# Zero matmuls ahead of the waits in the first retention head of a decoder trunk

## What is computed

```python
def retention_mixer(h, w_in, w_out):       # h = rmsnorm(x, g[0]), 512 x 1024
    proj = h @ w_in
    q, k, v, gate = jnp.split(proj, [H*RET_DK, 2*H*RET_DK, 2*H*RET_DK + H*RET_DV], axis=-1)
    q = rotary(q, pos)
    k = rotary(k, pos) * (RET_DK ** -0.5)
    ...
    def step(state, inp):                  # chunks of 128 tokens
        qc, kc, vc = inp
        inner = jnp.einsum('bhnd,bhmd->bhnm', qc, kc) * decay_mask[None]
        out = jnp.einsum('bhnm,bhme->bhne', inner, vc)
        ...
    y = rms_unit(y) * jax.nn.silu(gate)
    return y @ w_out
```

## Time and profile before

| | |
|---|---|
| time, median of 3 runs | 1361.86 us (1361.46 to 1362.64) |
| time of the profiled execution | 1362.79 us |
| its span, first to last instruction | 1360.8 us |
| PE busy | 1326.5 us, 97% of the span |
| DVE, ACT, POOL busy | 903.3, 555.8, 85.3 us |
| mean granted clock of PE | 0.992 of full speed |
| PE's share of the chain that ended last | 89% |

### The profile page before, as it was taken

The page is one execution under the profiler, slowest core; times in us unless marked ns, Lnnn a source line. Parts: engine busy times, 40 slices in busy tenths (PEclk is TensorE's granted clock), DMA queues, the critical chain, the costliest instruction groups (busy, mean ns, idle before and its releaser), DMA issues.

```text
span 1360.8 us, 19429 instructions
## 1 busy us (share of the span) xinstructions
PE 1326.5 (97%) x8028; PEld 1183.7 (87%) x8028; DVE 903.3 (66%) x951; ACT 555.8 (41%) x681; POOL 85.3 (6%) x129
## 2 busy tenths in 40 slices
PE   5989999999999999999999999999999999999997
PEld 4768888888889899999888889899788999998886
DVE  4977767774357788887233666667578888874342
ACT  4253434343334443443222455456354444443231
POOL 1000000000011000000000211221120000000001
PEclk8989999999999999999999999999999999999999
DMA  7161424226434333323224123223224233323221
GB/s 248 47 215 60 135 70 142 83 62 245 172 109 125 95 93 110 119 82 125 93 92 139 32 75 105 76 71 124 93 91 126 78 109 94 109 62 125 92 93 62
DMA packets 101055, 145.57 MB, mean 107 GB/s; under 512 B 3659, under 2 KB 77643, under 8 KB 100980
## 3 DMA queue, kind: packets, MB, share of 16 engines
q1 hardware_dynamic: 90816, 137.18, 31.0%
q10 hardware_dynamic: 10164, 7.32, 1.7%
HBM read 138.17 MB, written 8.41 MB: 108 GB/s over the span
## 4 chain that ended last, share of the span: by engine, by line
PE 89%; DVE 5%; POOL 2%; ACT 1%; issue 1%; DMA 1%; SPq 0%; ACTq 0%; DVEq 0%; POOLq 0%
PE ps L1819 29%; PE ps L1821 28%; PE ps L1820 28%; PE ps L2146 1%; DMA raw<-in_ret_w_in 1%; PE ps L1865 1%; POOL rstd L710 1%; PE ps L2168 1%; PE ps L2167 1%; PE ps L2156 0%; PE ps L2031 0%; ACT junk L794 0%; DVE tmp L1236 0%; DVE tmp L1254 0%; POOL spare_lo L734 0%
## 5 line engine op out<-in xcount | busy, mean ns | idle before, releaser
L1216 DVE TENSOR_TENSOR w_lo<-raw,w_hi 128x2048 fp32r<-128x2048 f32 (+1 forms) x69 | 143.4, 2078 | 202.0 <-ACT w_hi L785 170.1
L1819 PE MATMUL ps<-h_hi,w_hi 128*128 128x256 f32 (+1 forms) x688 | 224.8, 327 | 0.0
L1821 PE MATMUL ps<-h_hi,w_lo 128*128 128x256 f32 (+1 forms) x688 | 223.9, 325 | 0.0
L1820 PE MATMUL ps<-h_lo,w_hi 128*128 128x256 f32 (+1 forms) x688 | 223.9, 325 | 0.0
L1819 PE MATMUL ps<-w_hi,act_hi 128*128 128x512 f32 x536 | 209.5, 391 | 1.1 <-ACT tmp L1026 0.8
L1821 PE MATMUL ps<-w_hi,act_lo 128*128 128x512 f32 x536 | 208.8, 390 | 0.0
L1820 PE MATMUL ps<-w_lo,act_hi 128*128 128x512 f32 x536 | 208.7, 389 | 0.0
L785 ACT ACTIVATE w_hi<-raw 128x2048 fp32r<-128x2048 f32 x44 | 84.2, 1913 | 174.2 <-PE ps L1821 171.6
L1819 PEld LDWEIGHTS ps<-h_hi,w_hi 128*128 128x128 f32 x688 | 131.0, 190 | 10.7
L1821 PEld LDWEIGHTS ps<-h_hi,w_lo 128*128 128x128 f32 x688 | 131.0, 190 | 10.7
L1820 PEld LDWEIGHTS ps<-h_lo,w_hi 128*128 128x128 f32 x688 | 131.0, 190 | 10.4
(11 more groups left out here) (253 smaller groups left out, 2947.0 us busy)
## 6 DMA issues: line engine op xcount, KB each, us to landing
raw<-in_ffn_w_down SPq DMA_DIRECT2D x22, 1024.0 KB, 5.1
x<-in_ret_w_in SPq DMA_DIRECT2D x13, 1024.0 KB, 5.2
raw<-in_ffn_w_up SPq DMA_DIRECT2D x24, 512.0 KB, 4.4
raw<-in_ffn_w_gate SPq DMA_DIRECT2D x24, 512.0 KB, 3.9
raw<-in_ret_w_in SPq DMA_DIRECT2D x10, 1024.0 KB, 5.2
raw<-in_ret_w_out SPq DMA_DIRECT2D x8, 1024.0 KB, 5.1
raw<-in_diff_w_in SPq DMA_DIRECT2D x8, 1024.0 KB, 5.6
tmp<-in_ffn_w_gate SPq DMA_DIRECT2D x12, 512.0 KB, 3.9
```

The source lines that it names most:

```text
L1216: nc.vector.tensor_tensor(out_ap, whole, high.bitcast(F32), ALU.subtract).then_inc(done, 1)
L1819: nc.tensor.matmul(out_ap, a_hi, b_hi, start=start, stop=False, skip_group_check=shared)
L1820: nc.tensor.matmul(out_ap, a_hi, b_lo, start=False, stop=False, skip_group_check=shared)
L1821: return nc.tensor.matmul(out_ap, a_lo, b_hi, start=False, stop=stop, skip_group_check=shared)
```

## The change

Matmuls of a tile of zeros are added on PE. The tile, `zeros`, is bf16, 128 partitions by 512 columns, and one DVE instruction sets it to 0 near the start. One call of `fill(b, n)` issues n matmuls of 128x512 into bank b, each with a start and a stop of its own, and nothing reads the result. No instruction is removed and none of the others is reordered. There are 56 such matmuls: 14 before the first transposes, 6 between the first two transposed blocks, 8 ahead of and 8 behind the last transposed block, 4 ahead of the wait for `bias_cp`, and 16 ahead of T3 in head 0, behind the wait for `ret_u2_made`.

```diff
+            zeros = sb("zeros", [P, S], BF16, ret)
...
             nc.vector.memset(rel[BUCKETS:BUCKETS + 1, :], MASKED).then_inc(set_up, 1)
+            nc.vector.memset(zeros[:], 0.0).then_inc(zeros_made, 1)
...
+            def fill(b, n):
+
+                for _ in range(n):
+                    nc.tensor.matmul(bank(b), zeros[:, 0:P], zeros[:], start=True, stop=True)
+
+            pe.wait_ge(zeros_made, 1)
+            fill(6, 14)
             pe.wait_ge(const_in, 16)
             turn_rows(0, 0)
+            fill(6, 6)
             turn_rows(0, 1)
...
             left_product(0, "B11", "a", True, between=first_rows)
+            fill(6, 8)
             turn_rows(0, 3)
+            fill(6, 8)
             pe.wait_ge(ret_p1_copied, 2)
             left_product(0, "B21", "a", False)
...
             mm.then_inc(bias_mm, 1)
             pe.wait_ge(h_split, ST)
+            fill(0, 4)
             pe.wait_ge(bias_cp, 1)
             columns(unit(0, "Q"), unit(0, "Q") % 3, (6, 7))
...
                 pe.wait_ge(ret_u2_made, h + 1)
+                if h == 0:
+                    fill(2, 16)
                 left_product(h, "T3", "b", True)
```

More of the change, by code:

```diff
@@ L223, in build @@
         first_row = sem("first_row")
+        zeros_made = sem("zeros_made")
         first_hi_made = sem("first_hi_made")
```

## The result

The changed kernel takes 1364.41 us (median of 16 runs, 1362.07 to 1367.15), against 1361.76 us (median of 16 runs, 1360.23 to 1362.77) for the kernel before. The ratio is 1.0023, with a 95% interval of 1.0016 to 1.0030, so the kernel became slightly slower, by 2.65 us. The forecast was 1362.6 in a range of 1359.5 to 1365.2. The profiled execution took 1366.44 us, its span is 1364.4 us, 3.6 more than before.

What follows compares the result with a forecast made beforehand. PE bounds the kernel, busy 1326.5 of 1360.8 us, with early waits and cold clock costing time. Profiled: 1362.79 - 2.9 + 3.5 - 0.6 = 1362.8; median: 1362.5; forecast 1362.6, own range 1361.2 to 1363.9, widened to 1359.5 to 1365.2.

Steps and rivals of the forecast that it cites:

- the sixteen: 16 fills before T3 in head 0: nothing hides them, so they cost 16 x 0.22, +3.5 us.
- rival (c): A transfer or ACT holds DVE's train, so B21's 2.9 us do not reach the path: 1365.4 us; chance 0.08.
- The signs that were named: Clock 1.00 from 22 to 34 us, L1593 at 33.5, `inner_first` wait near 2.9, T3's end within 1 us of 90.23.
- The first twenty and the memset: 14 and 6 fills around the first transposed blocks, and the zeroing: hidden or absorbed by a later 2.03 us wait; cost 0, gain 0.
- The 8 and 8: Fills around the last transposed block fit in the waits and keep the clock up, so B21 runs warm: -2.9 us.
- The second cold stretch: Half clock around the scores and T3: its waits stay, its loss may shrink by 0 to 1.3 us, say -0.6.
- PE never waits after it: After T3, from 90.23 to 330 us, PE never stops, so T3's later start delays nothing else.
- Rival (a): The clock stays up through the two open waits before the scores: 1360.3 us profiled, 1359.7 median; chance 0.14.
- Rival (b): Zeros do not keep the clock up; B21 gains nothing and the 16 fills run cold: 1368.7 us; chance 0.05.
- Rival (d): The 16 fills are partly hidden, or the clock stays up and is also saved elsewhere: below 1359 us; chance 0.07.

## Why the prediction was right, and where its sizes were off

The time lies in the range, 1.8 us above the forecast, and a gain at B21 against a larger cost of the sixteen is what happened. It also lies 0.5 above the forecast's own range, which ended at 1363.9 (by its own terms 1363.8 on the profiled execution and 1363.5 on the median); what holds it is the part that was added for rival (c), which did not happen. That much is luck. The signs that were named came: the clock at 1.00 before and through B21, L1593 at 33.68, the wait for `inner_first` at 2.84 us, and T3's end at 90.98. With a ratio of 1.0023 the change is just past the bound of 0.2% up to which the forecast called it the same, by no more than its interval. Step by step:

- **The first twenty and the memset, 0.** Right within 0.7 us. The memset took 0.27 us and hid. The twenty do not hold the clock: it fell within the first 21 us in five of the seven profiles that have them (granted 0.50 from 9.4 to 11.7 in four, and from 14 to 20 in the fifth). That they are harmless when cold was wrong in one of the five, by 2 us, because there the clock fell at B11 and halved the matmuls of B11 and not only the fills. That they gain nothing was not quite right either, since a B11 that begins cold uncovers the eight behind it.
- **The 8 and 8, -2.9 us.** The mechanism was right in every part: covered, clock at 1.00, B21 in 5.7 us, 2.7 us earlier at L1593, carried to the end, the rival (c) is out. The size holds against the profiled execution alone (-2.95). Against the median it was 1.1, and the other profiles show why: with no fills near it B21 took 8.42, 7.00, 7.07 and 5.67 us, so the first one, the slowest of the four, had more to win than a usual execution. Four profiles can't say how often each length comes. The text noted that the profiled run lay 0.93 above the median, but scaled only the last term by it. This is the term that was mis-sized.
- **The sixteen, +3.5 us.** Right: 3.5 by the step from none to 32, and 3.3 to 3.6 by the pairs of profiles, 0.21 to 0.23 us each where the text took 0.22.
- **The second cold stretch, -0.6.** In the first profile it lasted 5.9 us from the scores at 78.38, against 6.1 before, so next to nothing was won. That is why the head lost 0.75 us in this profile, where the three terms add up to 0. In the second profile it lasted 3.3 us, and 4.5 in the second profile of the kernel before: the term belongs to the execution more than to the change.
- **"PE never waits after it".** Wrong at 318 us. The rows ended at 330 with PE always busy, but the load of y had less than a microsecond of slack in hand, which a full PE column doesn't show.
- **Not foreseen:** the late load, 1.5 us in the first profile and about 1 in the two others; and the attention's start, where the clock falls in some executions, perhaps 1.0 us of the median by the variant with six more fills. Of the measured 2.65 us, -1.1 + 3.5 makes 2.4. The sum does not close: the fall is also in one of the two profiles of before, but the late load is in neither, and its 1 us or more ought to stand in the 2.65 too. What makes up for it is not known; the 1.1 and the 2.65 were measured on different chips.
- **Rival (a)** did not happen: the clock fell at both open waits, in both profiles of the changed kernel. **Rival (b)** is out: zeros kept the clock up at B21, and in the runs with fills ahead of the waits of the first head at T3 too. **Rival (d)** is out: none of the sixteen was hidden.

## What to carry to other kernels

Work that keeps the clock up belongs in front of the wait, sized by the wait that the trace shows with a little to spare (here 0.2 to 0.4 us were left), and looked at again where the work ahead of it can run cold; behind the wait each such matmul costs about its own duration, here 0.2 us, and gives nothing back. Look at every wait of the matmul engine with the clock behind it, in several profiles, and not only at the longest, since a clock that falls in some executions is seen as scatter: here filling the waits of the first head and of the attention's start took off 4.0 us and cut the scatter from 2.5 us or more to 0.6. Before a gain is read off one profile, its time should be compared with the median, and the terms that hang on chance scaled with it.

## What the hardware showed that I had not expected

- The clock fell behind a wait of 1.7 us at the attention's start (granted 0.51 from 797.71 to 801.17), in six of the eleven profiles that have nothing in front of that wait, and in none of the three that have six zero matmuls there. The two profiles of before differ in it, and so do the two of the changed kernel. A longer wait did not always bring it down: behind 2.09 us before B21 it stayed up in the profile with only the fills ahead of the scores. And at the wait of 0.95 us for the bias it fell in the second profile of before (0.50 from 36.3 to 39.6), where it had not in the first.
- After the fall B21 stayed at half clock for 5.9 us in one execution and 2.7 us in another of the same program, with the same work before it and waits of 2.03 and 1.77 us before the last transposed block.
- With matmuls added at 80 us, time was lost at 310 us. In the three profiles where two issues took 2.1 to 2.35 us together in place of 0.88, a block of instructions (0.02 MB in the row) was fetched just ahead of them. That the one causes the other is not shown.
